# Latent tiles through the mixer's tail as one, two, one, with head units closer together and two score buffers

## The chip, the cores and the metric

The kernel runs on one core of one Trainium2 chip. The metric is the device time of one execution in microseconds, and the figure for a kernel is the median of its runs. Everything is 32-bit floating point.

## The reference, cut to what matters

The program is a two-layer model over 512 latent tokens and 256 context tokens of width 1024, six tiles of 128 tokens in all. Each layer has a mixer and then PEER, a channel mixer with product keys. PEER is what most of the time goes to:

```
def peer(h, wq, sub_keys, u_tab, v_tab):
    q = (h @ wq).reshape(T, P_HEADS, 2, P_DKEY // 2)
    s = jnp.einsum("thpd,hpnd->thpn", q, sub_keys)
    sv, si = lax.top_k(s, 16)                       # for each of 16 half heads, 128 keys
    cand = sv[:, :, 0, :, None] + sv[:, :, 1, None, :]
    fv, fi = lax.top_k(cand, 16)
    ...                                             # 8 heads x 16 = 128 experts for each token
    a = gelu(einsum("tkd,td->tk", u_tab[ib], hb)) * gb
    return einsum("tk,tkd->td", a, v_tab[ib])
```

The mixer of the first layer gives every latent tile four heads of differential attention over all 768 tokens (two softmaxes, the second subtracted) and four pairs of windowed heads over the context and the neighbouring latent tiles. Their output is normalised, projected with `e_w_out`, gated, added to x, normalised again (norm2) and goes to PEER.

## The kernel before, in words

**The expert loop.** `run_experts` handles a layer's tiles one after another, each in 128 slots; one slot is one expert for each of the tile's 128 tokens. In a slot GpSimd issues an indirect DMA (L2637) that gathers 128 rows of 2048 numbers (u and v of an expert, 1.05 MB) into one of eight `ring` buffers; VectorE forms the dot product with h (L2734); ScalarE makes gelu, the gate and a diagonal matrix (L2754, L2756, L2760); TensorE multiplies that with the v half into banks 0 and 1 (L2771, four instructions a slot). GpSimd may issue slot s when TensorE has spent slot s - 8. In the first layer there are 6 x 128 = 768 slots, in the second 512.

**What runs beside it.** Beside the first layer's loop all the latent tiles' mixer work is done. Every engine walks the same slots in order, and each piece of side work is pinned to a slot by a table: in a slot an engine first does the side work put there, and then its part of the slot's expert. No queue is reordered, so what waits holds up the experts behind it.

`HeadUnits` has 32 units, eight for each latent tile (four differential ones, "A", then four windowed ones, "B"). A unit that begins at slot b does, before the change: `score` on TensorE at b (L925), `find` (maximum) on VectorE at b + 3 (L970, L972, L974), `exp` on ScalarE at b + 4 (L998), for A `mix` on VectorE at b + 7 (L954 to L959), and rounds of `turn` (TensorE transposes, L913) from b + 8 (A) or b + 6 (B) every three slots, each with `copy` on ScalarE (L988) and `value` on TensorE (L901) two slots later; last `take` on VectorE (L944 or L947) five slots after the last turn. Within a slot TensorE does value, turn, score in this order, VectorE take, mix, find, and ScalarE copy, exp. Units begin 9 slots apart for the first latent tile and 15 slots apart from slot 73 on.

`LatentMixer` then treats each latent tile by itself, at slots 79, 199, 319 and 439: norm of the heads' output, transposes, eight column blocks of the output projection (L2042), gate and residual (L2078, L2080), norm2, transposes. All of these and the scores share PSUM bank 7. `LateScores` follows for the tile: 16 half heads, 4.4 slots apart, each with `query` (eight products, L1917), a copy (L1930), `score` (L1904) and a copy (L1937) into `sc`. Its weights and those of the projection pass through three buffers, filled by SyncE. `ChoicePlan` places the steps of a tile's top-16 search on VectorE (L1679 to L1716) in the 128 slots of the tile before. `NextFront` projects four tiles for the second layer from slot 440 on.

Of the kernel before, what the change touches and what calls it, by code (L numbers as in the profile page):

```python
# [820 lines left out]
class HeadUnits:  # L821
# [4 lines left out]
    def __init__(self, m, s, units, begin, probs, probsT, width, s_bank, s_banks, t_bank, o_bank):  # L826
# [12 lines left out]
        for n, (t, i) in enumerate(units):  # L839
            b, a_head = begin[n], i < A_HEADS  # L840
            parts = [(0 if a_head else c, j) for c in range(1 if a_head else 2) for j in range(len(self.blocks(n)))]
            self.at["score"].put(b, n)
            self.at["find"].put(b + 3, n)
            self.at["exp"].put(b + 4, n)
            if a_head:
                self.at["mix"].put(b + 7, n)
# [11 lines left out]
            self.end.append(at + 2)  # L858
# [817 lines left out]
def top16(dve, heads, values, src, spare, index):  # L1676
# [8 lines left out]
    for h in heads:  # L1685
        dve.match_replace(spare[:, h, :], values[:, h, 0:8], src[:, h, :], LOW)
    dve.drain()
    yield
    for h in heads:
        dve.max(values[:, h, 8:16], spare[:, h, :])  # L1690
    dve.drain()
    for h in heads:
        dve.max_index(index[:, h, 8:16], values[:, h, 8:16], spare[:, h, :])
# [21 lines left out]
def first_scores(nc, m, a, layer, tiles, pre):  # L1715
# [6 lines left out]
    with Stage(nc, f"es{layer}") as s:  # L1722
        qT = s.sb("qT", [P, 2, NTL * P])
        sc, rest = s.sb("sc", [P, NTL, NH, NK]), s.sb("rest", [P, NH, NK])
# [75 lines left out]
class LateScores:  # L1800
# [6 lines left out]
    def __init__(self, m, a, s, layer, groups, outs, out_slots, begin, pace, turned_of, q_banks, score_banks, place=None):  # L1807
# [18 lines left out]
        for g in range(len(groups)):  # L1826
            for c in range(outs):
                self.add_item(out_slots[g][c], last_use)
            for hh in range(NH):
# [5 lines left out]
                scored = slot + took + 2  # L1835
                self.add_item(scored, last_use)
                self.at["query_copy"].put(slot + took + 2, u)
                self.at["score"].put(scored, u)
                self.at["score_copy"].put(slot + took + 4, u)
                if place is None:  # L1840
                    self.at["store"].put(slot + took + 5, u)
                self.copied[u] = slot + took + 4
# [79 lines left out]
    def scalar(self, act, slot):  # L1922
# [8 lines left out]
        for u in self.at["score_copy"](slot):  # L1931
            n = len(self.tiles_of(u))
            act.wait_ge(self.used, self.item(u) + 1)
            if self.place is not None:
                sc, sc_read, t0 = self.place
                act.wait_ge(sc_read, self.tiles_of(u)[0] - t0)
                act.copy(sc[:, u % self.NH, :], m.ps[:, self.score_banks[u % ns], 0:P]).then_inc(self.late_ready, 1)  # L1937
                continue
# [14 lines left out]
class LatentMixer:  # L1953
# [4 lines left out]
    POST, PITCH, N2, LATE = 79, 120, 32, 44  # L1958

    def __init__(self, m, a, s, place):  # L1960
        self.m, self.a = m, a
        self.gain_gn, self.ss, self.rms = s.sb("gain_gn", [P, A_DV]), s.sb("ss", [P, A_HEADS]), s.sb("rms", [P, 1])
        self.scale, self.shift = s.sb("scale", [P, D]), s.sb("n2_shift", [P, D])
        self.hT = s.sb("hT", [P, KC, P])
# [7 lines left out]
        begin = [9 * k for k in range(2 * A_HEADS)] + [73 + 15 * k for k in range((XT - 1) * 2 * A_HEADS)]  # L1972
        self.heads = HeadUnits(m, s, units, begin, s.sb("probs", [P, 2, NT * P]), s.sb("probsT", [P, 2, BANK]), NT * P, 2, 3, 5, 6)
        out_slots, late_begin = [], []
        for x in range(XT):
            b = self.POST + self.PITCH * x
            assert self.heads.end[8 * x + 7] < b
            at = lambda name, d, item: self.at[name].put(b + d, item)
            at("gn_root", 0, x)
            at("gn_scale", 3, x)  # L1980
            for r in range(2):
                at("o_turn", 4 + 3 * r, (x, r))
                at("o_copy", 6 + 3 * r, (x, r))
            at("g1_load", 0, x)
            at("x_load", 8, x)
            at("n2_load", self.N2 - 1, x)
            out_slots.append([b + 10 + 11 * (c // 4) + 5 * (c % 4) // 2 for c in range(KC)])
            for c in range(KC):
                self.at["out"].put(out_slots[-1][c], (x, c))
            for r in range(2):  # L1990
                self.at["out_take"].put(out_slots[-1][4 * r + 3] + 3, (x, r))
                at("h_turn", self.N2 + 6 + 3 * r, (x, r))
                at("h_copy", self.N2 + 8 + 3 * r, (x, r))
            at("n2_square", self.N2, x)
            at("n2_scale", self.N2 + 4, x)
            at("n2_shift", self.N2 + 5, x)
            late_begin.append(b + self.LATE)
        self.late_at = {slot: x for x, slot in enumerate(late_begin)}
        self.late = LateScores(m, a, s, 0, [[CT + x] for x in range(XT)], KC, out_slots, late_begin, [4.4] * XT,
                               lambda tiles, k: self.hT[:, k, :], [7], [7], place)  # L2000

    def h_of(self, t):
        return self.m.H[:, t % 3, :]

# [6 lines left out]
    def sync(self, sp, slot):  # L2011
        for x in self.at["g1_load"](slot):
            if x:
                sp.wait_ge(self.h_ready, x)
            sp.dma_start(self.scale[:, :], rows(self.m.mods[0, 0:1, 2 * D:3 * D])).then_inc(self.scale_loaded, 16)
        for x in self.at["n2_load"](slot):
            sp.wait_ge(self.out_taken, 2 * x + 2)
            sp.dma_start(self.scale[:, :], rows(self.m.n2_scale[0])).then_inc(self.scale_loaded, 16)
        for x in self.at["x_load"](slot):
# [4 lines left out]
    def tensor(self, pe, slot):  # L2024
        m = self.m
        for x, r in self.at["o_turn"](slot):
            pe.wait_ge(self.gn_done, x + 1)
            if r:
                pe.wait_ge(self.o_copied, 2 * x + 1)
            for k in range(4):  # L2030
                c = (4 * r + k) * P
                tr = pe.transpose(m.ps[:, 7, k * P:(k + 1) * P], m.R[:, CT + x, c:c + P], m.ident[:, :])
            tr.then_inc(self.o_turned, 1)
        for x, c in self.at["out"](slot):
            v, r = x * (KC + LateScores.NH) + c, c // 4
            w = self.late.bufs[self.late.buffer[v]]
            self.late.wait_loaded(pe, v)
            pe.wait_ge(self.o_copied, 2 * x + 2)
            if r:
                pe.wait_ge(self.out_taken, 2 * x + 1)  # L2040
            for k in range(KC):
                mm = pe.matmul(m.ps[:, 7, c % 4 * P:(c % 4 + 1) * P], self.hT[:, k, :], w[:, k * P:(k + 1) * P],  # L2042
                               start=(k == 0), stop=(k == KC - 1), skip_group_check=True)
            mm.then_inc(self.late.used, 1)
        for x, r in self.at["h_turn"](slot):
            pe.wait_ge(self.h_ready, x + 1)
            if r:
                pe.wait_ge(self.h_copied, 2 * x + 1)
            for k in range(4):
                c = (4 * r + k) * P  # L2050
                tr = pe.transpose(m.ps[:, 7, k * P:(k + 1) * P], self.h_of(CT + x)[:, c:c + P], m.ident[:, :])
            tr.then_inc(self.h_turned, 1)
        if slot in self.late_at:
            pe.wait_ge(self.h_copied, 2 * self.late_at[slot] + 2)
# [3 lines left out]
    def vector(self, dve, slot):  # L2058
# [5 lines left out]
        for x in self.at["gn_scale"](slot):  # L2064
            o = m.R[:, CT + x, 0:A_HEADS * A_DV].rearrange("p (a d) -> p a d", d=A_DV)
            dve.wait_ge(self.gn_rooted, x + 1)
            dve.reciprocal(self.ss[:, :], self.ss[:, :])
            dve.drain()
            dve.tensor_tensor(o, o, self.ss[:, :].unsqueeze(2).broadcast_to([P, A_HEADS, A_DV]), ALU.mult)
# [3 lines left out]
        for x, r in self.at["out_take"](slot):  # L2073
            cols = slice(r * BANK, (r + 1) * BANK)
            dve.wait_ge(self.late.used, x * (KC + LateScores.NH) + 4 * r + 4)
            dve.wait_ge(self.x_loaded, 16 * (x + 1))
            dve.wait_ge(self.scale_loaded, 32 * x + 16)
            dve.tensor_tensor(m.ps[:, 7, :], m.ps[:, 7, :], self.scale[:, cols], ALU.mult)  # L2078
            dve.drain()
            add = dve.tensor_tensor(m.R[:, CT + x, cols], m.R[:, CT + x, cols], m.ps[:, 7, :], ALU.add)  # L2080
            add.then_inc(self.out_taken, 1)
        for x in self.at["n2_scale"](slot):
            dve.wait_ge(self.sq_done, x + 1)
            dve.wait_ge(self.scale_loaded, 32 * x + 32)
            dve.reciprocal(self.rms[:, :], self.rms[:, :])
            dve.drain()
            dve.scalar_tensor_tensor(out=self.h_of(CT + x), in0=m.R[:, CT + x, :], scalar=self.rms[:, :], in1=self.scale[:, :],
                                     op0=ALU.mult, op1=ALU.mult)
        for x in self.at["n2_shift"](slot):
            dve.drain()  # L2090
            dve.tensor_tensor(self.h_of(CT + x), self.h_of(CT + x), self.shift[:, :], ALU.add).then_inc(self.h_ready, 1)
        self.heads.vector(dve, slot)

    def scalar(self, act, slot):
        m = self.m
        for x in self.at["gn_root"](slot):
            act.wait_ge(self.heads.taken, 8 * (x + 1))
            if x:
                act.wait_ge(self.gn_done, x)
            for h in range(A_HEADS):  # L2100
                act.activation(m.ps[:, 7, h * P:(h + 1) * P], m.R[:, CT + x, h * P:(h + 1) * P], ACT.Square,
                               accum_out=self.ss[:, h:h + 1])
            act.drain()
            act.activation(self.ss[:, :], self.ss[:, :], ACT.Sqrt, bias=m.eps[:, :], scale=1.0 / A_DV).then_inc(self.gn_rooted, 1)
        for x, r in self.at["o_copy"](slot):
# [837 lines left out]
```

## Time and profile before

| | |
|---|---|
| median of three runs | 4542.93 us (4534.92 to 4543.4) |
| profiled execution, first to last instruction | 4536.7 us |
| granted TensorE clock, mean | 0.948 |
| PE busy | 3771.8 us, 83% |
| DVE, ACT, POOL busy | 2602.3, 1740.7, 1715.4 us |
| HBM read | 1551.50 MB |
| software DMA queue (the gathers) | 1342.36 MB |

The profiled execution's own time is its span and what the run adds around it; the median of the runs lies 6.2 us above that span. In the profile PE is TensorE, PEld its weight load, DVE VectorE, ACT ScalarE, POOL GpSimd and SP SyncE; L12 is line 12 of the kernel. The first layer's expert loop lies at about 561 to 2683 us of the span.

### The profile page before, as it was taken

What the parts mean: (1) busy time and instruction counts of PE and PEld (TensorE: products, weight loads), DVE (VectorE), ACT (ScalarE), POOL (GpSimd) and SP (SyncE); (2) the same over time, 40 slices, a digit from 0 to 9 for tenths busy, and PEclk for the clock granted to TensorE, in tenths of its full rate; (3) what the DMA queues carried; (4) which work ended last, traced back from release to release, by engine and by line L of the source; (5) the groups of instructions that cost most, each with busy time, mean ns of one, the idle gap of its engine ahead of it and who ended that gap; (6) DMA issues with size and microseconds to landing.
All of it is one profiled execution on the core that took longest, in us unless ns stands there. A gap on an engine that the chain in (4) does not pass through costs nothing. (4 is left out here: it accounts for less than half of the span.)

```text
span 4536.7 us, 43969 instructions
## 1 busy us (share of the span) xinstructions
PE 3771.8 (83%) x12422; PEld 1913.6 (42%) x12422; DVE 2602.3 (57%) x5662; ACT 1740.7 (38%) x5087; POOL 1715.4 (38%) x1358
## 2 busy tenths in 40 slices
PE   6987688899899898888889967675989997877777
PEld 2443544554455454444444423545444452222222
DVE  3533587656856856755654433335775557666544
ACT  1112155444544544433333322421664433333333
POOL 0100044434434444444444422000433534556675
PEclk9988899999999999999999988798999999999999
DMA  4363499999999999999999971014999999999998
GB/s 169 113 237 147 154 420 401 420 420 420 407 420 420 410 420 419 419 420 421 418 417 420 421 310 54 4 61 150 402 377 396 422 422 416 413 421 421 419 421 357
DMA packets 251863, 1564.87 MB, mean 345 GB/s; under 512 B 30946, under 2 KB 45186, under 8 KB 80228
## 3 DMA queue, kind: packets, MB, share of 16 engines
q0 software_dynamic: 185088, 1342.36, 71.7%
q1 hardware_dynamic: 64596, 216.23, 12.5%
q10 hardware_dynamic: 1936, 3.48, 0.2%
q8 instruction: 99, 1.62, 0.1%
q14 instruction: 144, 1.18, 0.1%
HBM read 1551.50 MB, written 10.46 MB: 344 GB/s over the span
## 5 line engine op out<-in xcount | busy, mean ns | idle before, releaser
L2771 PE MATMUL ps<-ex_ring,ex_diag 128*128 128x512 f32 x5120 | 2493.9, 621 | 506.1 <-ACT ex_diag L2760 481.6
L2637 POOL DMA_INDIRECT ex_ring<-in_p_uv,ex_expert x1280 | 1650.1, 1289 | 2014.0 <-PE ps L2771 1523.6
L2734 DVE SCALAR_TENSOR_TENSOR ex_ring<-ex_ring,H 128x1024 f32<-128x1024 f32 x1280 | 1561.7, 1225 | 1170.4 <-DMA ex_ring<-in_p_uv,ex_expert 1156.0
L2771 PEld LDWEIGHTS ps<-ex_ring,ex_diag 128*128 128x128 f32 x5120 | 924.6, 194 | 1728.9 <-ACT ex_diag L2760 916.5
L2754 ACT ACTIVATE ex_act_w<-ex_dots 128x1 f32<-128x1 f32 x1280 | 258.6, 202 | 1519.6 <-DVE ex_ring L2734 1512.6
L2760 ACT ACTIVATE ex_diag<-ident_sb,ex_weight 128x128 f32<-128x128 f32 x1280 | 514.6, 402 | 92.2 <-issue 5.4
L2756 ACT ACTIVATE ex_weight<-ex_act_w,ex_gates 128x1 f32<-128x1 f32 x1280 | 377.9, 295 | 90.6 <-issue 3.1
L685 PE MATMUL ps<-win_w,hT 128*128 128x512 f32 (+1 forms) x480 | 191.9, 557 | 1.9 <-PEq L281 1.4
L1917 PEld LDWEIGHTS ps<-bs_hT,bs_w 128*128 128x128 f32 x1024 | 127.4, 196 | 33.9 <-issue 33.9
L685 PEld LDWEIGHTS ps<-win_w,hT 128*128 128x128 f32 x480 | 90.3, 191 | 106.0 <-issue 103.8
L1917 PE MATMUL ps<-bs_hT,bs_w 128*128 128x128 f32 x1024 | 127.0, 278 | 0.3 <-issue 0.3
L1746 PE MATMUL ps<-hT,pre_w 128*128 128x256 f32 x512 | 115.6, 379 | 2.7 <-PEq L281 2.7
L461 POOL TENSOR_TENSOR R<-R,pout_tmp 128x512 f32<-128x512 f32 x8 | 10.1, 1265 | 267.6 <-DVEq L452 267.6
L2754 ACT ACT_TABLE_LOAD x72 | 92.4, 1283 | 47.1 <-DVE ex_ring L2734 45.9
L2734 DVE DVE_READ_ACCUMULATOR ex_ring<-ex_ring,H 128x1 f32 x1280 | 105.9, 83 | 0.0
L1746 PEld LDWEIGHTS ps<-hT,pre_w 128*128 128x128 f32 x512 | 95.0, 190 | 15.0 <-issue 3.3
L700 ACT ACTIVATE ph_sq<-ps 128x512 f32<-128x512 f32 (+1 forms) x24 | 12.4, 517 | 160.6 <-PE ps L685 160.6
L901 PEld LDWEIGHTS ps<-KV,bs_probsT 128*128 128x128 f32 x480 | 62.9, 192 | 24.0 <-issue 24.0
L418 PE MATMUL ps<-wout_w,hT 128*128 128x512 f32 x128 | 61.7, 644 | 13.5 <-DMA wout_w<-in_o_w_out 7.3
L2042 PEld LDWEIGHTS ps<-bs_w,bs_hT 128*128 128x128 f32 x512 | 63.4, 195 | 15.8 <-issue 15.8
L730 DVE TENSOR_REDUCE ph_ss<-ph_sq 128x8 f32<-128x512 f32 (+1 forms) x24 | 14.1, 586 | 96.2 <-ACT ph_sq L700 96.2
L1917 PE MATMUL ps<-K,bs_w 128*128 128x256 f32 x256 | 66.3, 382 | 0.0
(396 smaller groups left out, 3221.6 us busy)
## 6 DMA issues: line engine op xcount, KB each, us to landing
bs_w<-in_p_wqk SPq DMA_DIRECT2D x80, 576.0 KB
ca_mod_w<-in_w_mod SPq DMA_DIRECT2D x24, 1024.0 KB, 9.1
ex_ring<-in_p_uv,ex_expert POOLq DMA_INDIRECT x1280, 14.7
pre_w<-in_p_wqk SPq DMA_DIRECT2D x32, 576.0 KB, 3.7
win_mod_w<-in_w_mod SPq DMA_DIRECT2D x16, 1024.0 KB, 4.8
bs_w<-in_e_w_out_tiles SPq DMA_DIRECT2D x32, 512.0 KB
win_w<-in_e_w_in SPq DMA_DIRECT2D x9, 1024.0 KB, 11.3
mod_mod_w<-in_w_mod SPq DMA_DIRECT2D x8, 1024.0 KB, 13.1
```

What stands on the lines that cost most here:

```text
L418: mm = pe.matmul(m.ps[:, b, 0:chunk], m.hT[:, k, (t - m.h0) * P:(t - m.h0 + 1) * P], w[:, q, k, :], start=(k == 0), stop=(k == KC - 1))
L685: mm = pe.matmul(m.ps[:, u % 4, 0:halves * 256], m.hT[:, k, t * P:(t + 1) * P], pre.w[:, n % 2, 0:halves, k, :], start=(k == 0), stop=(k = ...
L901: mm = pe.matmul(self.O[:, cols], self.probsT[:, r % 2, x * P:(x + 1) * P], KV[:, self.blocks(n)[j], vals], start=(j == 0), stop=(j == las ...
L1746: mm = pe.matmul(m.ps[:, h % 2, 0:NTL * P], pre.w[:, h % RING, k * P:(k + 1) * P], m.hT[:, k, cols], start=(k == 0), stop=(k == KC - 1))
L1917: mm = pe.matmul(m.ps[:, self.q_banks[u % nq], 0:cols], w[:, j * P:(j + 1) * P], self.turned_of(self.tiles_of(u), j), start=(j == 0), stop ...
L2042: mm = pe.matmul(m.ps[:, 7, c % 4 * P:(c % 4 + 1) * P], self.hT[:, k, :], w[:, k * P:(k + 1) * P], start=(k == 0), stop=(k == KC - 1), ski ...
L2637: pool.indirect_dma_start(ring[:, r, :], None, uv_rows, bass.IndirectOffsetOnAxis(ap=expert[:, t % 2, n:n + 1], axis=0),).then_inc(landed[ ...
L2734: dve.scalar_tensor_tensor(out=ring[:, r, 0:D], in0=ring[:, r, 0:D], scalar=1.0, in1=h_of(t + t0), op0=ALU.mult, op1=ALU.mult, accum_out=d ...
L2754: act.activation(act_w[:, b:b + 1], dots[:, t % 2, n:n + 1], ACT.Gelu)
L2756: act.activation(weight[:, b:b + 1], act_w[:, b:b + 1], ACT.Copy, scale=gates[:, t % 2, n:n + 1])
L2760: act.activation(diag[:, b, :], m.ident[:, :], ACT.Copy, scale=weight[:, b:b + 1]).then_inc(diag_ready, 1)
L2771: mm = pe.matmul(mix_banks(t)[:, half, :], diag[:, b, :], ring[:, r, D + half * BANK:D + (half + 1) * BANK], start=(n == 0), stop=(n == SL ...
```

## The change: what it does

In the first layer's expert loop:

- Latent tiles go through the mixer's tail and the scores in groups [0], [1, 2], [3], which begin at slots 60, 226 and 360. A group of two uses 128x256 products for the queries, and both tiles for each weight block of the projection. Each weight is read three times, not four.
- Head units get the offsets `TIGHT`, and begin 6 slots apart (first tile), 10 (second and third tile, from slot 52), 15 (fourth, from slot 216).
- `sc` has two buffers, so that scores of the second tile of a group can wait there. To pay for it, `rest` is cut to four heads, `posf`, `part`, `partf`, `num` lie in it, the candidates' comparison goes through `sc`, and `sc_read` is given at its end.
- Where query and score share a bank, the query's copy comes one slot after the query (before: two), the score's copy three slots after it (before: four).
- In the second layer the expert loop gets the moved buffers with one `sc`.

```diff
+    LOOSE = {"find": 3, "exp": 4, "mix": 7, "turn_a": 8, "turn_b": 6, "gap": 3, "copy": 2, "take": 5}
+    TIGHT = {"find": 2, "exp": 3, "mix": 5, "turn_a": 6, "turn_b": 5, "gap": 2, "copy": 1, "take": 3}
...
-            at = b + (8 if a_head else 6)
+            at = b + (after["turn_a"] if a_head else after["turn_b"])
...
-                for name, d in (("turn", 0), ("copy", 2), ("value", 2)):
+                for name, d in (("turn", 0), ("copy", after["copy"]), ("value", 2)):
                     self.at[name].put(at + d, r)
-                at += 3
-            self.at["take"].put(at + 2, n)
+                last_turn = at
+                at += after["gap"]
+            self.at["take"].put(last_turn + after["take"], n)
...
-                self.at["query_copy"].put(slot + took + 2, u)
+                self.at["query_copy"].put(scored - (1 if self.shared else 0), u)
...
-                self.at["score_copy"].put(slot + took + 4, u)
+                self.at["score_copy"].put(copied, u)
...
-                act.wait_ge(sc_read, self.tiles_of(u)[0] - t0)
+                act.wait_ge(sc_read, self.tiles_of(u)[-1] - t0 + 1 - sc.shape[1])
...
-        begin = [9 * k for k in range(2 * A_HEADS)] + [73 + 15 * k for k in range((XT - 1) * 2 * A_HEADS)]
...
+        for g, xs in enumerate(groups):
+            b, n = post[g], len(xs)
+            put("g1_load", b, g)
+            for i in range(n):
+                put("gn_root", b + i, (g, i))
+                put("gn_scale", b + 2 + i, (g, i))
...
+            at, ahead = b + 6 + 4 * n, 4 // n
+            out_slots.append([at + (ahead + 2) * (c // ahead) + c % ahead for c in range(KC)])
...
+        n = 2 * A_HEADS
+        begin = [6 * k for k in range(n)] + [52 + 10 * k for k in range(2 * n)] + [216 + 15 * k for k in range(n)]
+        self.mixer = LatentMixer(m, a, s, place, [[0], [1, 2], [3]], begin, [60, 226, 360], [4.4, 4.4, 4.4])
...
-                first = max(free, load + 6)
+                first = max(free, load if direct(t) else load + 6)
...
-        sc, rest = s.sb("sc", [P, NH, NK]), s.sb("rest", [P, NH, NK])
+        sc, rest = s.sb("sc", [P, SCS, NH, NK]), s.sb("rest", [P, 4, TOPK * TOPK])
...
-                    dve.sem_inc(sc_read, 1)
...
+                    dve.sem_inc(sc_read, 1)
                     dve.scalar_tensor_tensor(out=num[:, 0, :], in0=num[:, 0, :], scalar=float(NK), in1=num[:, 1, :],
```

With these tables the column blocks of the projection lie at slots 70 to 79, 240 to 253 and 370 to 379, the late scores at 95 to 164, 273 to 342 and 395 to 464 (before: 123 to 193, 243 to 313, 363 to 433 and 483 to 553), and the last head unit ends at slot 331 (before 432).

## Rows read from the trace of the kernel before

**Rows 1.** The page, 40 slices of the span: what the DMA engines moved.

```profile
GB/s 169 113 237 147 154 420 401 420 420 420 407 420 420 410 420 419 419 420 421 418 417 420 421 310 54 4 61 150 402 377 396 422 422 416 413 421 421 419 421 357
```

**Rows 2.** The page, DMA issues of the shared weights: count, KB of each.

```profile
bs_w<-in_p_wqk SPq DMA_DIRECT2D x80, 576.0 KB
...
bs_w<-in_e_w_out_tiles SPq DMA_DIRECT2D x32, 512.0 KB
```

**Rows 3.** Windows, dot products alone (two records a slot): slots 0, 48, 212, 336, 512.

```profile
561.00:686.00 125.00, 58.65 (x97) 0.92 1.01 418
686.00:1138.00 452.00, 200.84 (x327) 0.96 1.01 415
1138.00:1491.50 353.50, 152.15 (x250) 0.96 1.01 416
1491.50:1995.50 504.00, 216.54 (x353) 0.96 1.01 417
1995.50:2683.00 687.50, 315.51 (x512) 0.98 0.99 411
```

**Rows 4.** Timeline of slots 18 to 25, all engines: start, length, instruction, idle before.

```profile
612.99 1.57 PE L925 MATMUL ps<-KV,R 64*128 64x256 f32 x8
...
614.73 1.75 DVE L972 TENSOR_REDUCE bs_top<-ps 128x2 f32<-128x1536 f32 x1
...
616.31 1.05 PE L901 MATMUL ps<-KV,bs_probsT 128*128 128x128 f32 x8
...
616.64 1.22 DVE L2734 SCALAR_TENSOR_TENSOR ex_ring<-ex_ring,H 128x1024 f32<-128x1024 f32 x1
...
618.92 0.38 PE L913 MATMUL ps<-ident_sb,bs_probs 128*128 128x128 f32 x2
...
619.13 3.60 PE L2771 MATMUL ps<-ex_ring,ex_diag 128*128 128x512 f32 x8
...
619.34 0.37 ACT L988 COPY bs_probsT<-ps 128x256 f32<-128x256 f32 x1 [0.40 <-PE ps L913]
...
619.73 1.28 ACT L998 ACT_TABLE_LOAD   x1
...
622.91 1.28 ACT L2754 ACT_TABLE_LOAD   x1
...
624.73 0.28 DVE L944 COPY R<-ps 128x128 f32<-128x128 f32 x1
624.84 0.40 ACT L2760 ACTIVATE ex_diag<-ident_sb,ex_weight 128x128 f32<-128x128 f32 x1
...
625.30 2.62 PE L2771 MATMUL ps<-ex_ring,ex_diag 128*128 128x512 f32 x4 [2.12 <-ACT ex_diag L2760]
...
626.92 1.22 DVE L2734 SCALAR_TENSOR_TENSOR ex_ring<-ex_ring,H 128x1024 f32<-128x1024 f32 x1
```

**Rows 5.** Timeline of PE: expert products behind the exponentials of three other units.

```profile
602.07 3.28 PE L2771 MATMUL ps<-ex_ring,ex_diag 128*128 128x512 f32 x4 [2.73 <-ACT ex_diag L2760]
...
693.74 0.70 PE L2771 MATMUL ps<-ex_ring,ex_diag 128*128 128x512 f32 x1 [2.06 <-ACT ex_diag L2760]
...
717.71 5.40 PE L2771 MATMUL ps<-ex_ring,ex_diag 128*128 128x512 f32 x8 [2.63 <-ACT ex_diag L2760]
```

**Rows 6.** Groups by form, 590 to 2690 us: queries and projection on PE, a window's maximum, bands and take on DVE.

```profile
L1917 PE MATMUL ps<-bs_hT,bs_w 128*128 128x128 f32 x1024 | 127.0, 278 | 0.3 <-issue 0.3
L2042 PE MATMUL ps<-bs_w,bs_hT 128*128 128x128 f32 x512 | 63.4, 278 | 0.0
...
L972 DVE TENSOR_REDUCE bs_top<-ps 128x2 f32<-128x1280 f32 x8 | 11.9, 1492 | 0.6
...
L970 DVE TENSOR_TENSOR ps<-ps,band_sb 128x256 f32<-128x256 f32 x24 | 9.6, 429 | 11.4 <-PE ps L925 11.3
...
L947 DVE TENSOR_SCALAR R<-ps,bs_rec 128x64 f32<-128x64 f32 x32 | 7.6, 280 | 1.2
```

More of the change, by code:

```diff
@@ L1953, with __init__ @@
 class LatentMixer:
[L1958 to L1962, printed above, removed]
+    LOAD = 5
+    def __init__(self, m, a, s, place, groups, begin, post, pace):
+        self.m, self.a, self.groups = m, a, groups
+        self.first = [sum(len(g) for g in groups[:n]) for n in range(len(groups) + 1)]
+        self.takes = [2 * n for n in self.first]
+        W = max(len(g) for g in groups)
+        self.gain_gn, self.ss, self.rms = s.sb("gain_gn", [P, A_DV]), s.sb("ss", [P, W, A_HEADS]), s.sb("rms", [P, W])
         self.scale, self.shift = s.sb("scale", [P, D]), s.sb("n2_shift", [P, D])
-        self.hT = s.sb("hT", [P, KC, P])
+        self.hT = s.sb("hT", [P, KC, W * P])
         (self.vec_loaded, self.scale_loaded, self.gn_rooted, self.gn_done, self.o_turned, self.o_copied, self.x_loaded, self.out_taken,
@@ L1974, in __init__ @@
+        put = lambda name, slot, item: self.at[name].put(slot, item)
         out_slots, late_begin = [], []
[L1975 to L1987, printed above, removed]
-            for c in range(KC):
[L1989 to L1997, printed above, removed]
@@ L2002, in h_of, with tile @@
+        self.late_at = {slot: g for g, slot in enumerate(late_begin)}
+        self.late = LateScores(m, a, s, 0, [[CT + x for x in xs] for xs in groups], KC, out_slots, late_begin, pace,
+                               lambda tiles, k: self.hT[:, k, 0:len(tiles) * P], [7], [7], place)
+        for g in range(len(groups) - 1):
+            assert self.late.copied[(g + 1) * LateScores.NH - 1] < post[g + 1]
     def h_of(self, t):
         return self.m.H[:, t % 3, :]
+    def tile(self, g, i):
+        return CT + self.first[g] + i
@@ L2025, in tensor @@
         m = self.m
[L2026 to L2029, printed above, removed]
+        for g, i, r in self.at["o_turn"](slot):
+            t, u = self.tile(g, i), 2 * (self.first[g] + i) + r
+            if i == 0 and r == 0:
+                pe.wait_ge(self.gn_done, self.first[g + 1])
+            else:
+                pe.wait_ge(self.o_copied, u)
             for k in range(4):
                 c = (4 * r + k) * P
-                tr = pe.transpose(m.ps[:, 7, k * P:(k + 1) * P], m.R[:, CT + x, c:c + P], m.ident[:, :])
+                tr = pe.transpose(m.ps[:, 7, k * P:(k + 1) * P], m.R[:, t, c:c + P], m.ident[:, :])
@@ L2033, in tensor @@
             tr.then_inc(self.o_turned, 1)
-        for x, c in self.at["out"](slot):
-            v, r = x * (KC + LateScores.NH) + c, c // 4
+        for g, c in self.at["out"](slot):
+            n = len(self.groups[g])
+            v, r, part = g * (KC + LateScores.NH) + c, c // (4 // n), c % (4 // n)
             w = self.late.bufs[self.late.buffer[v]]
             self.late.wait_loaded(pe, v)
-            pe.wait_ge(self.o_copied, 2 * x + 2)
+            pe.wait_ge(self.o_copied, 2 * self.first[g + 1])
@@ L2039, in tensor @@
             if r:
[L2040 to L2043, printed above, removed]
-            mm.then_inc(self.late.used, 1)
[L2045 to L2048, printed above, removed]
+                pe.wait_ge(self.out_taken, self.takes[g] + r)
@@ new lines, in tensor @@
+            for i in range(n):
+                at = (i * (4 // n) + part) * P
+                for k in range(KC):
+                    mm = pe.matmul(m.ps[:, 7, at:at + P], self.hT[:, k, i * P:(i + 1) * P], w[:, k * P:(k + 1) * P],
+                                   start=(k == 0), stop=(k == KC - 1), skip_group_check=True)
+            mm.then_inc(self.late.used, 1)
+        for g, i, r in self.at["h_turn"](slot):
+            t, u = self.tile(g, i), 2 * (self.first[g] + i) + r
+            pe.wait_ge(self.h_ready, self.first[g] + i + 1)
+            if i or r:
+                pe.wait_ge(self.h_copied, u)
@@ L2072, in vector @@
                 .then_inc(self.gn_done, 1)
[L2073 to L2078, printed above, removed]
+        for g, r in self.at["out_take"](slot):
+            n, t = len(self.groups[g]), self.tile(g, 0)
+            wide = BANK // n
+            cols, o = slice(r * wide, (r + 1) * wide), m.ps[:, 7, :].rearrange("p (x d) -> p x d", d=wide)
+            dve.wait_ge(self.late.used, g * (KC + LateScores.NH) + (r + 1) * (4 // n))
+            dve.wait_ge(self.x_loaded, 16 * self.first[g + 1])
+            dve.wait_ge(self.scale_loaded, 32 * g + 16)
+            dve.tensor_tensor(o, o, self.scale[:, cols].unsqueeze(1).broadcast_to([P, n, wide]), ALU.mult)
@@ L2079, in vector @@
             dve.drain()
-            add = dve.tensor_tensor(m.R[:, CT + x, cols], m.R[:, CT + x, cols], m.ps[:, 7, :], ALU.add)
+            add = dve.tensor_tensor(m.R[:, t:t + n, cols], m.R[:, t:t + n, cols], o, ALU.add)
             add.then_inc(self.out_taken, 1)
[L2082 to L2085, printed above, removed]
+        for g, i in self.at["n2_scale"](slot):
+            t = self.tile(g, i)
+            dve.wait_ge(self.sq_done, self.first[g] + i + 1)
+            dve.wait_ge(self.scale_loaded, 32 * g + 32)
+            dve.reciprocal(self.rms[:, i:i + 1], self.rms[:, i:i + 1])
@@ L2095, in scalar @@
         m = self.m
[L2096 to L2099, printed above, removed]
+        junk = self.hT[:, :, :].rearrange("p k c -> p (k c)")
+        for g, i in self.at["gn_root"](slot):
+            act.wait_ge(self.heads.taken, 8 * self.first[g + 1])
+            if g and i == 0:
+                act.wait_ge(self.gn_done, self.first[g])
             for h in range(A_HEADS):
-                act.activation(m.ps[:, 7, h * P:(h + 1) * P], m.R[:, CT + x, h * P:(h + 1) * P], ACT.Square,
-                               accum_out=self.ss[:, h:h + 1])
+                act.activation(m.ps[:, 7, h * P:(h + 1) * P], m.R[:, self.tile(g, i), h * P:(h + 1) * P], ACT.Square,
+                               accum_out=self.ss[:, i, h:h + 1])
@@ new lines, in scalar @@
+        for g, i, r in self.at["o_copy"](slot):
+            act.wait_ge(self.o_turned, 2 * (self.first[g] + i) + r + 1)
+            act.copy(self.hT[:, 4 * r:4 * r + 4, i * P:(i + 1) * P], m.ps[:, 7, :].rearrange("p (k c) -> p k c", c=P)).then_inc(self.o_copied, 1)
+        for g, i in self.at["n2_square"](slot):
+            act.wait_ge(self.out_taken, self.takes[g + 1])
+            act.activation(junk[:, i * D:(i + 1) * D], m.R[:, self.tile(g, i), :], ACT.Square, accum_out=self.rms[:, i:i + 1])
@@ L2116, in scalar @@
+        for g, i, r in self.at["h_copy"](slot):
+            act.wait_ge(self.h_turned, 2 * (self.first[g] + i) + r + 1)
+            act.copy(self.hT[:, 4 * r:4 * r + 4, i * P:(i + 1) * P], m.ps[:, 7, :].rearrange("p (k c) -> p k c", c=P)).then_inc(self.h_copied, 1)
         self.late.scalar(act, slot)
@@ L2167, in __init__ @@
         self.at["load"].put(self.NORM_AT[-1] + 6, 0)
-        self.at["load"].put(mixer.late.copied[XT * LateScores.NH - 1] + 1, 1)
+        self.at["load"].put(max(mixer.late.copied.values()) + 1, 1)
         assert slot + 6 < NT * SLOTS
@@ L2539, in __init__, with run_experts @@
             assert slot > shifted + 1 and slot < base + SLOTS - 2
-def run_experts(nc, m, a, layer, tiles, last, make_beside, h_of, ring_size, mixes, take_at):
+def run_experts(nc, m, a, layer, tiles, last, make_beside, h_of, ring_size, mixes, take_at, scs):
     T, t0 = len(tiles), tiles[0]
@@ L2651, in choose @@
                             dve.sem_inc(claimed, 1)
[L2652 to L2653 removed]
+                            yield from top16(dve, range(4 * q, 4 * q + 4), val, sc[:, t % SCS], head_rest, pos)
                     if not first:
```

148 lines of the change are left out of this document (83 added, 65 removed).

## The prediction

> **What bounds the kernel now.** I read first the page's 40 slices. From the sixth slice on, wherever the expert loops run, the DMA engines move 420 GB/s in most slices; a few slices show 401, 407 and 410 [rows 1]. A slot's gather is 128 x 8192 bytes = 1.049 MB, so 2.50 us at 420 GB/s, and the weights for the side work come on top. The windows cut at slots of the first layer's loop show the same: 411 to 418 GB/s, with two dot-product records a slot, so 2.6 us a slot in the first 48 slots and 2.7 to 2.9 later [rows 3]. By this view the loop is bound by bytes.
>
> The timeline of one head unit shows a second limit that lies just under it. At slots 17 to 22 TensorE has work without a pause (transposes, scores, values, experts) until it has to wait 2.12 us for the diagonal of slot 22 [rows 4]. The reason is on ScalarE: it may copy the second round of transposes only when TensorE has made them (618.92), then loads the table of exp (1.28 us), does two exponentials, loads gelu's table back (1.28 us), and only then makes the diagonal that TensorE gets at 625.30 [rows 4]. The same wait stands behind the exponentials of other units, 2.73, 2.06 and 2.63 us, and from one to the next it is 23.2 us (602.07 to 625.30, type A) and 24.0 us (693.74 to 717.71, type B) [rows 4, 5]. Nine slots are between them: 2.58 and 2.66 us a slot, already more than the gather's 2.50. So at a pitch of nine slots bytes and this loop of waits bind at nearly the same rate.
>
> **The loop worked out.** Lengths at full clock, from start to next start [rows 4]: an expert slot on TensorE 1.72 us (3.44 for two), two transposes 0.21, so four 0.44, an A unit's scores 1.50, eight value products 0.89, four 0.45 (half). An A unit at nine slots: 9 x 1.72 + 0.44 + 0.21 + 1.50 + 0.89 + 0.45 = 19.0, plus the wait 2.1 = 21.1. Measured is 23.2; the rest is clock: four expert products behind a wait take 3.28 and 2.62 us, eight take 5.40 where eight take 3.60 otherwise [rows 4, 5], and the granted clock of this window is 0.92 [rows 3]. I take 1.5 us for each wait of 2 us or more. The Trainium skill, "TensorE: Matmul & The Clock Gate", section on HAM oscillation, says that recurring pauses of TensorE send it back to half clock each time; the trace agrees, with the 5.40 us beside 3.60. Without any such loss my final sum would be about 60 us smaller.
>
> **What the change removes.** One pass over the weights. This layer makes 64 of the 80 loads of 576 KB (the other 16 are the second layer's) and all 32 of 512 KB [rows 2]; a fourth of both is 13.6 MB. One gate row and one norm row, loaded for each group and no longer for each tile, are another 1.0 MB. At 420 GB/s 35 us. TensorE's products are the same number of columns (a pair's query is 128x256), so nothing goes there. This is worth 35 us only where bytes bind.
>
> **What pitch and offsets do.** Nothing is reordered, so I follow the chains.
>
> A, six slots apart. Copy 2 of the unit before and exp of this unit now both lie in slot b + 3, and turn 2 in slot b + 2. Behind turn 2 TensorE has one expert (1.72) until it needs the diagonal of b + 3; turn 2 to that diagonal takes 6.38 (618.92 to 625.30) [rows 4]. Wait: 6.38 - 0.21 - 1.72 = 4.4. Then value 2 in b + 4; in b + 5 VectorE's take waits for it, then mix (2.3 with the take, 624.73 to 626.92 and a little), the dot product 1.3, ScalarE 1.15 to the diagonal: 4.8, while TensorE has one expert: wait 3.1. Before, these lay two slots apart. A unit is 6 x 1.72 + 3.5 + 4.4 + 3.1 = 21.3, with two clock losses 24.3 us. B, six apart: no mix; copy 2 in b + 2 and the diagonals of b + 2 and b + 3 in a row, 0.6 + 0.9 + 5.5, while TensorE has two experts and a value round (4.3): wait 2.7; 6 x 1.72 + 3.65 (turns 0.88, values 1.78, scores two thirds of A's) + 2.7 = 16.7, with one loss 18.2.
> Slots 0 to 47: first unit 17, 3 x 24.3, 4 x 18.2 = 163 us, now 125 [rows 3]. **+38** (+22 without clock losses).
>
> A, ten apart (slots 52 to 91, 132 to 171). Find in b + 2 needs the scores of b: 2.0 for the maximum and bias, 1.3, 1.0 against two experts: wait 1.0. Then exp, 5.5 from diagonal to diagonal against one expert: 3.8. 17.2 + 3.5 + 4.8 + 1.5 = 27.0. B, ten apart, with five blocks and three rounds: the take of the unit before falls into the slot of find, b + 2, ahead of it, and waits for the last value round in TensorE's b + 1. Behind that: take 0.66, two bands 0.86, maximum 1.49 [rows 6], small steps 0.5, dot 1.3, ScalarE 1.0 = 5.8, against one expert: wait 4.1; exp: 4.1 more. 17.2 + 4.6 (turns 1.1, values 2.2, scores 1.3) + 8.2 + 3.0 = 33. The late scores, 18 x 0.124 = 2.2 us of TensorE every 4.4 slots [rows 6], lie partly in the waits; I count 0.7 of them, 3.5 us for ten slots, in slots 95 to 164. The projection, 128 x 0.124 = 16 us, counts 0.8.
> Slots 48 to 211: 10 + (108 + 17) + 4 x 36.5 + (108 + 11) + 4 x 33 = 532 us. By bytes it would be 446 (172 MB of gathers, 15 MB of weights and rows); now 452 [rows 3]. **+80** (+25 without clock losses and with late work wholly in the waits: A 25.5 or the bytes, B 30).
>
> Fifteen apart (216 to 335): A 35.6, B 35.9. The pair's projection (256 x 0.124 = 32, at 0.8) and pair queries (4.4 us every 4.4 slots, 12 a unit): 10 + 142 + 26 + 4 x 47.5 = 368, now 353.5. **+15** (0 to +25). This is where TensorE's own load, 3.0 us a slot, passes the bytes' 2.83.
>
> Slots 336 to 511: no heads; bytes bind: 184.6 MB of gathers and 18 MB of weights and rows, 483 us, and 7 as an allowance for the search of the loop's fourth tile, whose last 18 steps now lie in 22 slots. 490, now 504: **-14**. Slots 512 to 767: the nine weight blocks that now still come there (late scores up to 553) are gone, 5.3 MB or 12.6 us: 675, now 687.5: **-12**. The 35 us are thus in the sums; only in the last two do they show.
>
> **At nothing.** The waits for `sc_read` with two buffers: the search of a tile ends 20 slots or more before scores are written over it. The later `sc_read` in the second layer: SyncE gets it some 14 us later once, and its scores are first wanted in slot 8. For other tiles the search before is over ahead of slot 128. The moved small tiles cost the same instructions. SyncE's queue loses 24 weight loads and two row pairs; the projection's fourth and eighth block (slots 73, 79) have their weights issued only three slots ahead, up to 2 us each, inside the range. The query's copy one slot earlier holds ScalarE to one slot ahead of TensorE; a diagonal needs 1.0 us and an expert lasts 1.72, so it costs only beside an exp (rival 3).
>
> **Sum.** +38 + 80 + 15 - 14 - 12 = +107 on the profile's span 4537 (median of the runs 6 us above it). I round 4650 down for late work that hides: **4640 us**. Its own range is 4590 to 4680; all the lower bounds together (+22 + 25 + 0 - 26) give 4564.
>
> **Rivals.**
> 1. Bytes bind throughout (chance 0.09). The slices at 420 GB/s speak for it [rows 1]; against it stands that TensorE already waits at nine slots with 2.58 us a slot [rows 4]. 4543 - 35 = 4508 us. It decides if a unit six slots apart takes under 15.7 us. "Perfetto Trace Analysis" of the Trainium skill, section on the most-contended engine, says to work on the busiest resource first, which is the DMA here; by that rule the time would be this one.
> 2. Only the six-slot stretch binds, and at ten slots the waits hide behind bytes (0.09): 38 - 35 = +3, 4546 us, range 4530 to 4570. It needs B units of ten slots in 25 to 28 us; for it: late units before lay beside heads at full 415 GB/s [rows 3].
> 3. The shared bank adds its own waits (0.14): a pair's query (3.5 us) and its copies hold ScalarE to one slot ahead, so each exp beside them costs another 4 us; 11 units lie beside late scores, +45: 4685 us.
> The forecast has 0.68.
>
> A measurement of this kernel tells 0.2% (9 us) from no change. Faster: rival 1, 0.09. Same: part of rival 2, 0.05. Slower: 0.86. The range is 4565 to 4695: below it lie rival 1 and most of rival 2 (0.16), above it a little of rival 3.
>
> **What would show it.** In the changed profile: slots 0 to 47 in 150 to 170 us at 310 to 340 GB/s, with PE waits of 3 to 4.5 us behind L2760's diagonal twice a unit; slots 48 to 211 in 500 to 540 us; slots from 336 on at 415 GB/s or more and shorter than now; 14.6 MB less read. I am wrong if the first 48 slots stay near 125 us (the chain through take and mix is then not what I follow), or if in slots 92 to 131 VectorE's take does not wait for values.

## The result, and the profile after

The changed kernel takes 4686.8 us (median of 4 runs, 4685.36 to 4693.28), the kernel before 4541.4: 1.0315 times as long, 95% interval 1.0286 to 1.0344. Forecast were 4640 us, range 4565 to 4695, slower with 0.86. Direction and main mechanism came as forecast; the loss is 145 us where 100 were said. The page of the changed kernel (answers to [rows 1]):

```profile
span 4685.0 us, 43338 instructions
...
GB/s 163 117 243 134 194 303 343 368 341 357 328 366 371 355 389 416 420 420 414 421 421 418 421 421 150 4 1 141 334 369 392 422 422 420 397 421 421 420 421 356
...
HBM read 1536.82 MB, written 10.46 MB: 330 GB/s over the span
```

From the sixth slice to the fifteenth, where the heads are, the DMA engines move 303 to 389 GB/s and no longer 420; behind the heads it is 420 again. 14.7 MB less are read. The windows, cut at slots 0, 48, 212, 336 and 512 as in [rows 3], dot products alone:

```profile
564.00:731.00 167.00, 57.54 (x96) 0.87 0.86 322
731.00:1258.50 527.50, 194.63 (x329) 0.91 0.89 349
1258.50:1666.50 408.00, 146.69 (x247) 0.96 0.92 360
1666.50:2154.00 487.50, 215.39 (x354) 0.98 1.01 417
2154.00:2828.00 674.00, 315.47 (x512) 0.98 0.99 411
```

Against [rows 3] that is +42, +75, +54.5, -16.5 and -13.5 us; forecast were +38, +80, +15, -14 and -12. TensorE's timeline of slots 8 to 17, with the waits of two A units six slots apart (answers to [rows 5]):

```profile
592.29 1.88 PE L2814 MATMUL ps<-ex_ring,ex_diag 128*128 128x512 f32 x4
598.46 3.17 PE L2814 MATMUL ps<-ex_ring,ex_diag 128*128 128x512 f32 x4 [4.28 <-ACT ex_diag L2803]
601.42 1.06 PE L906 MATMUL ps<-KV,bs_probsT 128*128 128x128 f32 x4
602.27 2.01 PE L2814 MATMUL ps<-ex_ring,ex_diag 128*128 128x512 f32 x4
607.13 1.98 PE L2814 MATMUL ps<-ex_ring,ex_diag 128*128 128x512 f32 x4 [2.85 <-ACT ex_diag L2803]
...
615.85 1.98 PE L2814 MATMUL ps<-ex_ring,ex_diag 128*128 128x512 f32 x4
621.79 2.62 PE L2814 MATMUL ps<-ex_ring,ex_diag 128*128 128x512 f32 x4 [3.96 <-ACT ex_diag L2803]
...
625.05 2.56 PE L2814 MATMUL ps<-ex_ring,ex_diag 128*128 128x512 f32 x4
629.91 3.62 PE L2814 MATMUL ps<-ex_ring,ex_diag 128*128 128x512 f32 x4 [2.29 <-ACT ex_diag L2803]
```

There are two waits a unit, 4.28 and 2.85 us, then 3.96 and 2.29, where 4.4 and 3.1 were worked out; before there was one of 2.1 to 2.7 [rows 4, 5]. Where the second comes from is seen in the later unit, all engines (this view has three of the four last products):

```profile
625.29 0.29 DVE L949 COPY R<-ps 128x128 f32<-128x128 f32 x1 [7.33 <-PE ps L906]
...
627.56 1.22 DVE L2777 SCALAR_TENSOR_TENSOR ex_ring<-ex_ring,H 128x1024 f32<-128x1024 f32 x1
...
629.45 0.40 ACT L2803 ACTIVATE ex_diag<-ident_sb,ex_weight 128x128 f32<-128x128 f32 x1
...
629.91 2.93 PE L2814 MATMUL ps<-ex_ring,ex_diag 128*128 128x512 f32 x3 [2.29 <-ACT ex_diag L2803]
```

VectorE stands 7.33 us in take (L949) until TensorE has done a value round, then mixes, and only then makes the next dot product, from which ScalarE makes the diagonal that TensorE waits for. What VectorE waited for in slots 0 to 335 (us in total, times, longest), now and, in the last two lines, before:

```profile
DVE R L952 <- PE ps L906: 151.1, 16, 17.1
DVE R L949 <- PE ps L906: 120.3, 16, 14.0
DVE ex_ring L2777 <- DMA ex_ring<-in_p_uv,ex_expert: 58.0, 29, 5.7
...
DVE ex_ring L2734 <- DMA ex_ring<-in_p_uv,ex_expert: 243.4, 192, 5.5
DVE R L944 <- PE ps L901: 10.6, 3, 3.7
```

All 32 takes wait, 271 us in all; before, three did, 10.6 us. Waiting for gathers, the sign of a loop bound by bytes, is down from 243 to 58 us.

### The profile page after: what moved, and what is told of

It is laid out like the page before. It is cut to its first block and busy times, and to the rows that moved or that the text cites. A ratio compares the mean times of both kernels' runs of the same rounds, so it can differ in the third digit from the quotient of the medians.

```text
span 4685.0 us, 43338 instructions
## 1 busy us (share of the span) xinstructions
PE 3813.3 (81%) x12166; PEld 1906.7 (41%) x12166; DVE 2589.7 (55%) x5662; ACT 1734.8 (37%) x5071; POOL 1716.1 (37%) x1358
## 3 DMA queue, kind: packets, MB, share of 16 engines
q1 hardware_dynamic: 60852, 201.54, 11.5%
## 5 line engine op out<-in xcount | busy, mean ns | idle before, releaser
L2814 PE MATMUL ps<-ex_ring,ex_diag 128*128 128x512 f32 x5120 | 2524.1, 627 | 612.9 <-ACT ex_diag L2803 581.9
L1923 PEld LDWEIGHTS ps<-bs_hT,bs_w 128*128 128x128 f32 x768 | 113.8, 196 | 31.3 <-issue 25.2
L1923 PE MATMUL ps<-bs_hT,bs_w 128*128 128x128 f32 (+1 forms) x768 | 122.8, 314 | 0.0
L993 ACT COPY bs_probsT<-ps 128x512 f32<-128x512 f32 (+1 forms) x72 | 37.0, 514 | 147.2 <-PE ps L918 147.0
L1936 ACT COPY bs_qT<-ps 128x128 f32<-128x128 f32 (+1 forms) x64 | 20.1, 313 | 144.3 <-PE ps L1923 144.3
L418 PE MATMUL ps<-wout_w,hT 128*128 128x512 f32 x128 | 61.7, 645 | 13.6 <-DMA wout_w<-in_o_w_out 7.2
```

The costliest lines, as they stand in the source:

```text
L418: mm = pe.matmul(m.ps[:, b, 0:chunk], m.hT[:, k, (t - m.h0) * P:(t - m.h0 + 1) * P], w[:, q, k, :], start=(k == 0), stop=(k == KC - 1))
L1923: mm = pe.matmul(m.ps[:, self.q_banks[u % nq], 0:cols], w[:, j * P:(j + 1) * P], self.turned_of(self.tiles_of(u), j), start=(j == 0), stop ...
L2814: mm = pe.matmul(mix_banks(t)[:, half, :], diag[:, b, :], ring[:, r, D + half * BANK:D + (half + 1) * BANK], start=(n == 0), stop=(n == SL ...
```

## The experiments

For every run the time of the slot blocks, from the start of the dot product of a block's first slot to that of the next block's (the last to slot 767), and the run's time. Runs marked * are single executions; the others are medians of 4 to 12 executions (before: 23). Of those 23 executions 20 lie within 8 us of their median and three 10 to 23 us above it, so a difference of some 10 us to a single execution is not told from chance by its total. The blocks are each from one profiled execution: in stretches that an edit leaves alone they differ by 2 to 5 us (changed against late_copies and spread in the first two blocks).

| kernel | 0-47 | 48-211 | 212-335 | 336-511 | 512-767 | us |
|---|---|---|---|---|---|---|
| before | 124.7 | 452.2 | 353.4 | 504.0 | 680.1 | 4541 |
| changed | 166.6 | 527.3 | 408.2 | 487.7 | 666.2 | 4687 |
| take4 | 149.5 | 510.5 | 395.5 | 487.3 | 667.1 | 4639 |
| no_gelu * | 141.0 | 481.6 | 370.9 | 485.8 | 666.3 | 4578 |
| loose | 124.6 | 451.8 | 357.4 | 504.3 | 677.4 | 4548 |
| offsets * | 148.5 | 477.6 | 367.1 | 509.9 | 676.9 | 4613 |
| offsets_take5 * | 141.2 | 464.0 | 359.1 | 504.7 | 675.9 | 4578 |
| single * | 164.7 | 532.8 | 367.0 | 500.6 | 677.4 | 4670 |
| late_copies * | 164.1 | 521.9 | 407.0 | 486.0 | 667.4 | 4673 |
| spread * | 164.1 | 523.1 | 402.0 | 497.0 | 666.9 | 4687 |
| last_pair | 124.6 | 487.9 | 347.6 | 487.9 | 667.6 | 4550 |
| last_pair_11 | 124.7 | 465.9 | 344.8 | 488.9 | 667.2 | 4527 |
| last_pair_12 | 124.8 | 468.3 | 344.3 | 491.0 | 666.1 | 4527 |

**take4**

```diff
-    TIGHT = {..., "copy": 1, "take": 3}
+    TIGHT = {..., "copy": 1, "take": 4}
```

> The changed kernel with one number changed: in the tight offsets a head unit's result is taken four slots after its last turn, not three. Theory of the loop of waits: at a pitch of six slots an A unit's take and mix no longer stand in the slot behind the second value round that TensorE does late, so the second wait of 3.1 us and its clock loss go (3 units, some 14 us in slots 0 to 47); at a pitch of ten a B unit's take leaves the slot of the next unit's find, 2.4 us for each of 8 units, 19 us. Together some 33 us less than the changed kernel, about 4650 us. Rival, the pair of tiles and the shared bank cost the time: within 5 us of 4687.

Measured 4638.9 us, 1.0205 of before (1.0169 to 1.0242): 48 us less than the changed kernel for one number. Slots 0 to 47 gave 17 (expected 14), 48 to 211 17 (19); the other 13 came in 212 to 335, which I had not counted on. The parts differ from what was expected too: of the first 17 us only 11.5 came in the A units' slots, 0 to 23, and of the second some 13 in the B units', 92 to 131 and 172 to 211, where all 19 were expected. VectorE's waits in take (slots 0 to 335) fell from 271 to 113 us, and part of them moved to find (L975):

```profile
DVE ps L975 <- PE ps L930: 82.2, 16, 12.0
...
DVE R L952 <- PE ps L906: 60.8, 8, 14.7
DVE R L949 <- PE ps L906: 51.9, 12, 9.0
```

**no_gelu**

```diff
-  act.activation(act_w[:, b:b + 1], dots[:, t % 2, n:n + 1], ACT.Gelu)
+  act.activation(act_w[:, b:b + 1], dots[:, t % 2, n:n + 1], ACT.Copy if layer == 0 else ACT.Gelu)
```

> The changed kernel with gelu left out in the first layer's expert loop (a copy in its place), so that ScalarE loads no table for it; the output is not the reference's. Theory of the loop: two table loads of 1.28 us leave the chain from copy to diagonal of every head unit, with part of the clock loss behind the waits: 32 units, 2.5 to 3.5 us each in slots 0 to 335, so 70 to 100 us less, 4590 to 4620 us. Rival, bytes or TensorE's own load bind: at most 15 us less.

Measured 4577.8 us, 109 less and somewhat more than expected. The bytes are the same, and so is TensorE's work; over slots 0 to 335 TensorE's waits for the diagonal fell from 189.4 to 119.3 us (changed kernel first), of which some 26 are at the loop's start in both. The chain through ScalarE sets the time in these slots: 25.6, 45.7 and 37.3 us came out of the first three blocks, 3.4 us for each of 32 units where two table loads are 2.6 us, and 2 us out of the last two.

```profile
PE ps L2814 <- ACT ex_diag L2803: 189.4, 71, 26.7
...
PE ps L2814 <- ACT ex_diag L2803: 119.3, 71, 25.4
```

**loose**

```diff
-  begin = [6 * k for k in range(n)] + [52 + 10 * k ...] + [216 + 15 * k ...]
+  begin = [9 * k for k in range(n)] + [73 + 15 * k for k in range(3 * n)]
-  LatentMixer(m, a, s, place, [[0], [1, 2], [3]], begin, [60, 226, 360], [4.4, 4.4, 4.4])
+  LatentMixer(m, a, s, place, [[0], [1], [2], [3]], begin, [79, 199, 319, 439], [4.4] * 4)
-  HeadUnits.TIGHT)
+  HeadUnits.LOOSE)
```

> The changed kernel with the loose offsets, the old spacing of the head units (9 and 15 slots) and each latent tile by itself at the old slots 79, 199, 319, 439; what stays changed are the two score buffers, the moved small tiles, the later read signal, the copies of the late scores one slot earlier and the tighter tail. Theory of the loop: all the loss comes from spacing, offsets and the pair, so 4541 us, within 10. Rival, the buffers, the copies beside the shared bank or the denser projection blocks cost: 4560 or more.

Measured 4547.7 us, 1.0011 of before (0.9995 to 1.0026). At the old spacing and offsets, the buffers, the later read signal, the copies and the tail cost nothing that can be told; it is spacing, offsets and grouping that bring the 145 us.

**offsets**

```diff
 (against loose)
-  HeadUnits.LOOSE)
+  HeadUnits.TIGHT)
```

> The kernel loose with the tight offsets: spacing 9 and 15, each tile by itself, only the offsets differ from it. Loop theory: the maximum comes two slots after the scores and the exponentials three, so a unit has waits of 1.0 and 3.8 us where it had 2.1; at nine slots that is 19.0 + 4.8 + 1.5 to 3 = 25.5 to 27 us where it took 23.3, some 16 us over eight units; at 15 slots the bytes hide it. 4555 to 4565 us. Rival, the offsets cost nothing without the spacing: 4541 to 4548 us.

Measured 4612.8 us: +65, four times what I expected. The offsets alone cost nearly half of the loss, at the old spacing. VectorE's waits in slots 0 to 335:

```profile
DVE R L952 <- PE ps L906: 100.0, 12, 10.7
DVE R L949 <- PE ps L906: 99.1, 13, 13.5
```

My expectation counted find and exp and left out take. It lies one slot after its value round, so VectorE may be only one slot ahead of TensorE whenever it comes to a take, however far apart the units are. At nine slots an A unit's take also falls into the slot of the next unit's find.

**offsets_take5**

```diff
 (against offsets)
-    TIGHT = {..., "take": 3}
+    TIGHT = {..., "take": 5}
```

> The kernel offsets (old spacing, each tile by itself, tight offsets) with take five slots after the last turn, as the loose set has it. The kernel offsets takes 4613 us, 65 more than loose, and its VectorE stands 130 us in take waiting for TensorE's value round, which lies one slot before. If that closeness is what costs, this falls to 4550 to 4570 us (slots 0 to 47 from 148 to 130 or less). If it is find and exp one slot earlier, it stays above 4590.

Measured 4577.9 us: 35 us less than offsets, 30 more than loose, between the two answers; slots 0 to 47 fell to 141.2 us and not to 130. Take is a little over half of what the offsets cost. VectorE's waits show what went: some 20 us in take and not 199. They also point at find, one slot nearer to the scores: its waits (L975, L977) are up from 19 in loose to 90. But exp, mix, turn, gap and copy are still tight as well; no run changes find alone, so that the rest is find's is not shown.

```profile
DVE ps L975 <- PE ps L930: 55.7, 11, 10.2
DVE bs_top L977 <- PE ps L930: 33.9, 9, 6.8
DVE R L952 <- PE ps L906: 13.9, 7, 4.9
```

**single**

```diff
-  [[0], [1, 2], [3]], begin, [60, 226, 360], [4.4, 4.4, 4.4])
+  [[0], [1], [2], [3]], begin, [79, 199, 319, 439], [4.4] * 4)
```

> The changed kernel with every latent tile by itself at the old slots 79, 199, 319, 439 and its heads as changed (tight offsets, 6, 10 and 15 slots apart). It parts the pair from the spacing. If the 408 us of slots 212 to 335 come from the pair's doubled TensorE work beside heads, they fall to 350 to 365 here; if the tight offsets at 15 slots cost by themselves, they stay above 385. Slots 0 to 47 stay at 167, slots 48 to 211 at 495 to 530; the fourth weight pass comes back: 4630 to 4660 us in all.

Measured 4670.0 us, somewhat over the expected 4630 to 4660. Slots 212 to 335 take 367.0 us and not 408.2, at 408 GB/s and not 360 (dot products alone; below it all engines, of this kernel and then of the changed one):

```profile
1263.10:1630.00 366.90, 148.72 (x249) 0.96 1.00 408
...
1263.10:1630.00 366.90, 324.56 (x1259) 182.38 (x1258) 237.09 (x536) 169.79 (x506) 146.58 (x126) 0.96 1.00 408
...
1258.30:1666.60 408.30, 361.54 (x1338) 208.59 (x1337) 217.51 (x444) 184.84 (x541) 148.42 (x127) 0.96 0.92 360
```

So the pair beside heads costs 41 us there, and 37 of them are time in which TensorE is busy (361.5 and not 324.6 us). It gives back 13 in slots 336 to 511 and 11 in 512 to 767; the whole run is 17 us longer with the pair. In the changed kernel slots 240 to 255 hold all eight double blocks of the projection:

```profile
1341.60:1413.10 71.50, 67.75 (x373) 47.40 (x372) 28.64 (x53) 21.91 (x64) 20.51 (x20) 0.98 0.92 345
```

TensorE is busy 67.75 of 71.5 us. Here hardly any latency is left to hide; it is TensorE's own work. The larger part of the 41 us lies behind it, beside the pair's queries: slots 276 to 335 take 202.6 us and not 172.0. The edit also moves the tails of the single tiles, so 17 us is the price of the grouping with its slots, not of the pair alone.

**spread**

```diff
-  out_slots.append([at + (ahead + 2) * (c // ahead) + c % ahead for c in range(KC)])
+  out_slots.append([at + (ahead + 2) * (c // ahead) + c % ahead if n == 1 else at + 3 * c for c in range(KC)])
```

> The changed kernel with the pair's eight projection blocks three slots apart (slots 240 to 261) and not two in every four (240 to 253); norm and scores follow eight slots later. If the blocks cost because TensorE is full in those 14 slots and VectorE's take of them stops the dot products, slots 240 to 275 fall from 122 to 105 to 112 us, the whole by 8 to 15 us. If it is their sum that counts, no difference within 5 us.

Measured 4686.8 us, no change. Slots 240 to 255 fell from 71.5 to 52.9 us and 256 to 275 rose from 50.9 to 74.0. The projection's sum counts, not its density. The norm and scores moved with it: slots 276 to 335 took 191.8 and not 202.6 us, and slots 336 to 511 took 9 us more.

**late_copies**

```diff
-  copied = scored + (1 if self.shared else 2)
-  self.at["query_copy"].put(scored - (1 if self.shared else 0), u)
+  copied = scored + 2
+  self.at["query_copy"].put(scored, u)
```

> The changed kernel with the late scores' two copies back in their old slots (query's two, score's four slots after the query). If the copies in the shared bank hold ScalarE so close to TensorE that each exp beside them costs more (rival 3 of the prediction, 45 us), slots 96 to 163 and 276 to 343 get 20 us or more shorter. If the loop through the head units alone sets the time, within 8 us of the changed kernel, 4680 to 4692.

Measured 4673.2 us, 14 less, between the two answers. But slots 0 to 47 and 48 to 71, which hold no late score, took 164.1 and 61.7 us here and in spread, and 166.6 and 66.5 in the profile of the changed kernel, so 7 of the 14 are no effect of the copies. Of the two stretches that the expectation named, slots 96 to 163 did not move (234.9 us, 234.8 in the changed kernel), and 276 to 343 took 213.7 and not 225.4. ScalarE's waits for the query's products halved (108 to 52 us in slots 0 to 335), but those for the transposes rose from 147 to 186. Late scores beside heads gave at most 7 in all: rival 3 at 45 us does not stand.

**last_pair, last_pair_11, last_pair_12**

```diff
 last_pair (against the changed kernel)
+  begin = [9 * k for k in range(n)] + [73 + 11 * k for k in range(3 * n)]
+  LatentMixer(m, a, s, place, [[0], [1], [2, 3]], begin, [79, 190, 350], [4.4] * 3), HeadUnits.LOOSE
 last_pair_11 (against last_pair): the edit of late_copies
 last_pair_12 (against last_pair_11)
+  begin = [9 * k for k in range(n)] + [73 + 12 * k for k in range(9)] + [181, 191, 201, 211, 221, 233, 245, ...]
+  [79, 190, 352]
```

> The changed kernel with the loose offsets, units 9 slots apart for the first tile and 11 from slot 73 on, and groups [0], [1], [2, 3] at slots 79, 190 and 350, so that the pair has no heads beside it. Theory of the loop: an A unit of 11 slots takes 11 x 1.72 + 3.5 + 2.1 + 1.5 = 26 us and with late work 30.5, about the bytes' 31; the pair's projection costs some 8 us; the third weight pass saved gives its 35 us: 4515 us (4500 to 4530). Rival, a pair of tiles costs by itself (bank, copies, TensorE's load): 4560 or more.

Measured 4550.1 us, 1.0011 of before (0.9993 to 1.0029); the 35 us did not come, and the time lies between the two answers. Slots 212 to 767 gave 34 against before; slots 48 to 211 took 36 back. ScalarE's waits for the query's products in slots 92 to 211 were 66.5 us:

```profile
ACT bs_qT L1936 <- PE ps L1923: 66.5, 16, 5.7
```

> The kernel last_pair with the late scores' copies back in their old slots. In last_pair slots 92 to 211 took 374 us where loose takes 339, and ScalarE stood 163 us waiting for the query's products. If the copies hold ScalarE too close to TensorE, 15 to 30 us of that go: 4515 to 4530 us. If eleven slots are too few beside late scores whatever the copies do, 4540 to 4550.

Measured 4527.0 us, 0.9977 of before (0.9961 to 0.9993), as expected and some 10 us faster than before. The same wait is 19.2 us, and slots 48 to 211 take 465.9 us and not 487.9:

```profile
ACT bs_qT L1936 <- PE ps L1923: 19.2, 7, 5.4
```

Here, where the spacing was chosen to bring the loop just to the bytes' rate, the slot of a copy is worth 22 us; in the changed kernel, far from it and with the tight offsets, at most 7.

> As last_pair_11, but the head units stand 12 slots apart beside late scores and 10 where there are none (slots 181 to 220 and 293 to 333), the pair at slot 352. A unit of 12 slots beside late scores needs 27.7 us and 5 to 6 for the late work, 33 to 34, and the bytes 33.8: so both ends of the loop meet. 4510 to 4525 us, below both kernels. If the pair itself costs what it saves: 4541.

Measured 4527.0 us, 0.9983 of before (0.9967 to 0.9999), the same as with 11 and 2 us outside the expected range. Slots 48 to 211 still take 16 us more than before; a slot more between the units beside late scores did not close this, and what holds it there stays open.

## Why the prediction was right, and where it was off

- **Bytes are not the bound at six and ten slots.** Right: 322 and 349 GB/s in the first two blocks. Rival 1 gave 4508 us, and a six-slot A unit would have had to take under 15.7 us; the first takes 23.3 (598.46 to 621.79) where 24.3 were worked out.
- **Slots 0 to 47, +38.** Measured +42. The two waits are there, 4.28 and 2.85 where 4.4 and 3.1 were worked out. Slots 0 to 23, the A units, take 90.2 us (forecast 90), slots 24 to 47, the B units, 76.5 (73).
- **Slots 48 to 211, +80.** Measured +75, but partly by luck, since errors of both signs cancel: the slots of the first four A units take 125.3 us (forecast 125), those of the B units with late scores 136.0 (146), of the next A units 128.4 (119), of the last B units 123.9 (132). A units' takes wait at ten slots too (19.8 us in slots 52 to 91); I had priced that wait for B units only.
- **Slots 212 to 335, +15.** This is the mis-sized term: +55 were measured, and single splits it. 14 us are there without the pair (367.0 against 353.4): at 15 slots I gave the tight offsets no price but one wait of 1.0 and one of 3.8 us, and none for take; take4 got 13 us back there, and in offsets the block is 10 us longer than in loose. The other 41 are the pair. By the prediction's own lengths the block without the pair would have been about 335 us (an estimate: heads and start 294, one tile's projection 13, its queries 28), below the 351 that 124 slots need at 2.83 us. So half of the pair's 33 us was thought to vanish in a gap up to the bytes' rate. That gap was not there: single takes 367.0. Nor did a fifth of the pair's work hide: 33 us stand for it at the factor 0.8, 41 were measured.
- **Slots 336 on, -26.** Measured -30. The weights' 35 us come where no heads are, and only there. Of the signs named, two fail as they stand: slots 512 to 767 move 411 GB/s and not 415, as they did before [rows 3], and a unit's second wait is 2.3 to 2.9 us and not 3 or more.
- **The clock.** 1.5 us for each wait was about right as a mean: the granted clock of the first block fell from 0.92 to 0.87, and a single wait cost between 0.1 and 1.7 us (last section).
- **At nothing:** buffers and read signal, confirmed by loose at the old spacing. **Rival 2** fell: the ten-slot stretch lost 75 us. **Rival 3** gave 4685 us, almost the measured time, but by chance: its mechanism, the copies beside the shared bank, gave at most 7 of its 45 us, and in slots 96 to 163 none.

What the runs give for the 145 us, taken in one order: loose against before 6, inside its interval; offsets against loose 65; spacing at those offsets 57 (single against offsets); the pair 17 (changed against single). These are differences of successive runs, so they add up by construction, and each that rests on a single execution is known to some 10 us. In another order the shares may differ: no run has the new spacing with the loose offsets.

## What to carry to other kernels

Where in-order engines walk a common list of slots, write the chain from engine to engine and back as a cycle, add its lengths and divide by the slots between two units: that rate, beside the rate of bytes, says whether closer spacing is free. The distance between a piece of work and the piece that consumes it on another engine is not slack to be trimmed: it is how far one engine may run ahead, and one slot of it, at one place, was worth 48 us here. The cycle must hold every such step: take was missing from it at 15 slots and in the expectation for offsets, which was four times too small. A saved transfer counted only in stretches that bytes bind; put the merged work where nothing else fills the engine that does it. Before you let added work vanish in a gap under the busiest resource, check that the stretch as changed, without that work, still has the gap.

## What was not expected of the hardware

What a wait costs in TensorE's clock does not follow its length. In the timeline above four products took 3.17 us behind a wait of 4.28, 2.62 behind 3.96 and 1.98 behind 2.85, where 1.88 is usual, but 3.62 behind the shortest wait, 2.29. Windows of the same stretch show the granted clock (the third number from the end):

```profile
599.20:602.50 3.30, 3.30 (x8) 1.76 (x8) 0.00 (x0) 0.13 (x1) 0.06 (x1) 0.50 1.03 429
...
626.50:629.80 3.30, 1.11 (x3) 0.19 (x1) 3.21 (x13) 0.84 (x3) 1.16 (x1) 1.00 0.87 293
629.90:633.20 3.30, 3.29 (x4) 1.40 (x5) 3.27 (x12) 0.90 (x3) 0.00 (x0) 0.50 0.89 305
```

After the 4.28 us wait, and again after the 2.29 us one, the clock is at half (0.50, that is 1.2 GHz); during the 2.29 us wait it is at full. So in neighbouring slots the price of a wait varied between 0.1 and 1.7 us; what decides it these runs do not show.
